# Start addresses in on-chip memory: pads at three places, and one product's moving operands set 32 bytes in front of a 128-byte boundary

## The reference, cut to what matters

```
u = rmsnorm(x, g_mix);  z = u @ w_in                        # mix: 2048 x 7184
y = concat(hgrn2 heads, gla heads)                          # gated recurrences, 12 heads
h = x + y @ w_out                                           # out: 2048 x 2048
m = rmsnorm(h, g_mlp) @ w_up                                # up: 2048 x 8192
h = h + square(relu(m)) @ w_down                            # down: 8192 x 2048
gate = sigmoid(rmsnorm(h, g_ple) @ w_pg)                    # gate: 2048 x 2048
h = h + gate * (p @ w_pp);  out = rmsnorm(h, g_final)
```

## Time and profile before

| | |
|---|---|
| median of three runs | 2427.51 us (2427.02 to 2428.92) |
| the profiled execution, its own time | 2428.29 us |
| its span | 2426.6 us |
| PE busy | 2393.7 us, 99% of the span, 13375 matmuls |
| weight loads (PEld) busy | 2082.1 us, 86% |
| DVE busy | 1939.1 us, 80% |
| ACT busy | 1202.9 us, 50% |
| granted TensorE clock | 0.998 of full speed (2.4 GHz) on the mean |

### The profile page before, as it was taken

How to read it: one execution, slowest core, us unless ns; L and a number is a source line. 1 busy time by engine, 2 the same in 40 slices (tenths; PEclk the granted TensorE clock), 3 DMA queues, 4 the chain that set the end, 5 groups by cost and what they waited for, 6 DMA issues and landing times.

```text
span 2426.6 us, 34798 instructions
## 1 busy us (share of the span) xinstructions
PE 2393.7 (99%) x13375; PEld 2082.1 (86%) x13375; DVE 1939.1 (80%) x2589; ACT 1202.9 (50%) x1787; POOL 50.7 (2%) x79
## 2 busy tenths in 40 slices
PE   8999999999999999999999999999999999999997
PEld 6888888888777888999999999988888888888885
DVE  6777777788887447988888888899999999995456
ACT  6445444444445235666666666643333333345345
POOL 4000000000000000000000000000000000000111
PEclk9999999999999999999999999999999999999999
DMA  6323323333324234666666666697564575633322
GB/s 176 87 73 82 86 70 85 87 84 81 79 74 152 92 131 137 182 204 200 199 197 196 197 196 196 205 353 253 198 232 160 191 257 195 229 131 116 112 85 99
DMA packets 381406, 373.71 MB, mean 154 GB/s; under 512 B 5532, under 2 KB 311352, under 8 KB 379224
## 3 DMA queue, kind: packets, MB, share of 16 engines
q1 hardware_dynamic: 381240, 371.88, 48.0%
q10 hardware_dynamic: 32, 0.01, 0.0%
HBM read 304.76 MB, written 67.11 MB: 153 GB/s over the span
## 4 chain that ended last, share of the span: by engine, by line
PE 62%; DVE 4%; ACT 1%; issue 1%; DMA 1%; DVEq 0%; ACTq 0%; SPq 0%
PE bank L2323 20%; PE bank L2325 20%; PE bank L2324 20%; DVE w_lo L2064 1%; DMA ring<-in_w_down 0%; DVE h L2110 0%; DVE w_lo L1927 0%; ACT w_hi L1143 0%; DVE w_lo L2201 0%; PE bank L2708 0%; PE bank L2603 0%; DVE gate_e L2227 0%; DVE h L2230 0%; PE bank L2401 0%; ACT gate_inv L1355 0%
## 5 line engine op out<-in xcount | busy, mean ns | idle before, releaser
L2323 PE MATMUL bank<-u_hi,w_hi 128*128 128x512 f32 x896 | 361.8, 404 | 3.4 <-DVE w_lo L1466 2.0
L2323 PE MATMUL bank<-w_hi,forms 128*128 128x512 f32 x896 | 349.4, 390 | 1.1 <-DVE h L2110 1.1
L2325 PE MATMUL bank<-u_hi,w_lo 128*128 128x512 f32 x896 | 349.8, 390 | 0.0
L2324 PE MATMUL bank<-u_lo,w_hi 128*128 128x512 f32 x896 | 349.2, 390 | 0.0
L2325 PE MATMUL bank<-w_hi,forms 128*128 128x512 f32 x896 | 348.7, 389 | 0.0
L2324 PE MATMUL bank<-w_lo,forms 128*128 128x512 f32 x896 | 348.6, 389 | 0.0
L2323 PE MATMUL bank<-xs,w_hi 128*128 128x256 f32 x1024 | 289.9, 283 | 1.4 <-DVE w_lo L1927 0.9
L2324 PE MATMUL bank<-xs,w_hi 128*128 128x256 f32 x1024 | 289.6, 283 | 0.0
L2325 PE MATMUL bank<-xs,w_lo 128*128 128x256 f32 x1024 | 289.5, 283 | 0.0
L1273 ACT ACTIVATE w_hi<-ring 128x1024 fp32r<-128x1024 f32 x124 | 132.0, 1066 | 214.6 <-PE bank L2325 140.4
L1466 DVE TENSOR_TENSOR w_lo<-w_raw,w_hi 128x2048 fp32r<-128x2048 f32 x70 | 160.0, 2286 | 63.2 <-ACT w_hi L874 63.0
(11 more groups left out here) (315 smaller groups left out, 5235.1 us busy)
## 6 DMA issues: line engine op xcount, KB each, us to landing
w_raw<-in_w_in SPq DMA_DIRECT2D x56, 1024.0 KB, 5.6
forms_scratch<-stage SPq DMA_DIRECT2D x32, 1792.0 KB, 11.4
forms<-forms_scratch SPq DMA_DIRECT2D x56, 1024.0 KB, 8.3
ring<-in_w_down SPq DMA_DIRECT2D x39, 1024.0 KB, 5.3
w_raw<-in_w_up SPq DMA_DIRECT2D x32, 1024.0 KB, 7.8
raw<-in_w_up SPq DMA_DIRECT2D x32, 1024.0 KB, 8.0
w_raw<-in_w_down SPq DMA_DIRECT2D x25, 1024.0 KB, 5.1
ring<-in_w_pg SPq DMA_DIRECT2D x18, 1024.0 KB, 5.0
```

Source lines behind the costliest of these rows:

```text
L2323: pe.matmul(ps, whi, xhi, start=start, stop=False, skip_group_check=shared)
L2324: pe.matmul(ps, whi, xlo, start=False, stop=False, skip_group_check=shared)
L2325: return pe.matmul(ps, wlo, xhi, start=False, stop=stop, skip_group_check=shared)
```

## The change: pads and offsets

A helper `aligned` allocates a byte tensor up to the next multiple of 128 that leaves at least 32 bytes of room in front. It is called ahead of u_hi, between u_hi and u_lo, and ahead of y. The tensors xs, xd and x11 of the up stage start 32 bytes (`SKEW`) in front of the regions' starts; xs gets a gap of 128 bytes between its two planes, so that the second starts 32 bytes in front of a multiple of 128 too. The other tensors laid out by `at` keep their offsets from region0 and region1, and move with them.

The pads before u_hi and between u_hi and u_lo move everything behind them by 128 and 256 bytes, from one multiple of 128 to another. The pad before y has 32 bytes and moves region1 from a remainder of 96 to 0. With remainders before and after as in the table above, every engine's instructions, their order and their waits are the same in both programs; only addresses differ.

```diff
+LINE, SKEW = 128, 32
...
-        region0 = -(-nc.sbuf_base // 64) * 64
+        def aligned(name, room):
+            start = -(-nc.sbuf_base // 32) * 32
+            end = -(-(start + room) // LINE) * LINE
+            if end > start:
+                sb(name, [P, end - start], U8)
+            assert nc.sbuf_base % LINE == 0
+            return nc.sbuf_base
+
+        region0 = aligned("pad0", SKEW)
         u_hi = sb("u_hi", [P, KT, S], F32R)
+        aligned("pad2", SKEW)
         u_lo = sb("u_lo", [P, KT, S], F32R)
...
-        region1 = nc.sbuf_base
+        region1 = aligned("pad1", SKEW)
         y = sb("y", [P, KT, S], stack=reg1)
...
-        xs = at("xs", region0, [P, 2, 4, 2, 2, 2, HALF], F32R)
-        xd = at("xd", region1, [P, 2, KT // 2, 2, HALF], F32R)
-        x11 = at("x11", region1 + KT * D, [P, KT // 2, 2, HALF], F32R)
+        xs = at("xs", region0 - SKEW, [P, 2, KT * S + LINE // 4], F32R)[:, :, 0:KT * S]\
+            .rearrange("q a (n j i l s) -> q a n j i l s", n=4, j=2, i=2, l=2)
+        xd = at("xd", region1 - SKEW, [P, 2, KT // 2, 2, HALF], F32R)
+        x11 = at("x11", region1 + KT * D - SKEW, [P, KT // 2, 2, HALF], F32R)
```

## The result

The changed kernel takes 2448.74 us (median of 6 runs, 2447.81 to 2451.48) against 2428.07 us before: ratio 1.0087, 95% interval 1.0077 to 1.0097. It is 20.7 us slower. The forecast was 2420.0 us with a range up to 2426. The profiled execution has a span of 2446.6 us against 2426.6.

The account below looks back on a forecast made before the run. The prediction took PE's pace, how fast one matmul follows another, as the bound. Up 4.5, gate 2.2 and mix 0.8 summed to 7.5 us off 2427.5, giving 2420.0 us, with an 8-in-10 range of 2416.5 to 2426.

Parts of the forecast that it names:

- u_hi, forms and all weight slots keep remainder 0: no change: Out and down stages: these operands' remainders stay 0, so no time was expected to change.
- the prediction's own sign of being right: Out and down must keep their lengths, 192 and 614 us, to within half a microsecond.
- a stationary operand at 96 costs 6.7 ns: Gate stage: steps with x1 or x2 at 96 take 233.3 ns a matmul, against 226.7 with x3 at 0.
- Up, 4.5 us: Up stage: xs going from 0 to 96 brings its products to 2.84 us, 4.5 us off over 32 pairs.
- Gate, 2.2 us: Gate stage: x1 and x2 going from 96 to 0 bring steps from 5.60 to 5.44 us, 2.2 us off.
- Mix, 0.8 us: Mix stage, float32 matmuls: 1.0 us gained by moving operands going to 0, less 0.2 for A at 32.
- the prediction's own sign of being wrong: Mix growing by more than 1 us, which would mean remainder 32 for A, V and norm costs the bounded 0.9.
- DVE, ACT, transfers at nothing: Vector and scalar work and transfers: addresses give 0, as small differences lie behind PE's work.
- the slower one: Rival: xs at 96 disturbs weight loads in up, up to 6.7 ns a matmul, 2445 us; chance 0.05.
- Nothing, by place in memory: Rival: pace depends on the part of memory a tensor lies in, not its remainder; 2427.5 us, chance 0.12.
- The rule of 16-byte lines: Whole kernel: remainders 0, 32 and 96 all start on a 16-byte line, so the time stays 2427.5 us.

Follow-up runs that it names:

- e1: The kernel before with one pad of 128 bytes in front of u_hi, so all tensors move up together: 2426.98 against 2428.25 us, ratio 0.9994.
- the second map: The kernel before with offsets and pads giving each stage another distance (mix -64, out +64, down +96, xd 0): 2447.11 us, ratio 1.0077.

## Why the prediction was wrong

- *Where it failed*: the step "u_hi, forms and all weight slots keep remainder 0: no change". The remainder was taken modulo 128 and of each operand alone. What counts is the difference of the two starts modulo 256 (in a stream whose matmuls all have the same one), and the pads of 128 and 256 bytes moved it from 0 to 128 for forms, x3 and u_hi. Down paid 13.8 us and out 4.4 (5.8 with the lower clock) where the sum had 0 and the prediction's own sign of being right was that both keep their length to half a microsecond. The readings of the rows were right, but the prediction read a rule of each operand's own remainder out of them ("a stationary operand at 96 costs 6.7 ns"), where they fit a distance of +32 and -32 as well. The kernel before had no float32r stream at a distance of 128, so its trace could neither show nor exclude this; the step took as given what it should have bounded, with 6.7 ns a matmul from the earlier trace rows on the 2688 of down, 18 us.
- *Up, 4.5 us*: right for the second plane of xs (2.84 us a product). The first plane went to a distance of +96, not -32, and stayed at 2.88. With both at -32 up lost 5.2 us (639.0 against 644.2).
- *Gate, 2.2 us*: x1 and x2 gained as said, 1.7 us when done alone. In the changed kernel x3 and p's tiles lost what they gained.
- *Mix, 0.8 us*: the stage grew by 2.6 us, the prediction's own sign of being wrong (more than 1 us), but for u_hi at 128 from w_hi and not for the float32 tiles. The streams lost more (229.0 against 227.3 ns a matmul, 4.6 us), and shorter waits gave part of it back (11.6 against 13.3 us). The gain from the float32 matmuls did not come: sixteen ql,kl take 1.95 us after the change as before it, where 1.92 was named. The term rested on a difference of 1.5 ns between 1.67 us over 15 distances (which is 111.3 ns, not 111.5) and 0.33 us over 3, and a row is rounded to 0.01 us, 3 ns in the second. Mix as a whole can't decide such a size: e1, which changes no distance, is 1.6 us shorter in mix than before as well, so differences of that size in this stage mean nothing.
- *DVE, ACT, transfers at nothing*: nothing speaks against it; DVE's busy time in up is 563.48 us in both kernels, and down came back to 614.5 us with forms alone set back.
- *The rivals*: the slower one named 2445 us, near the 2448.7 measured, but that is luck: its mechanism (xs disturbs the loads in up) is wrong, as up got faster. "Nothing, by place in memory" is refuted by xd in the second map and by xs at 2.84 in the low part of memory. The rule of 16-byte lines in the Trainium skill ("SBUF — State Buffer", Specifications (TRN2)) would have had the time unchanged; 0 against 128 bytes of distance, both multiples of 16, gave 5.44 and 5.58 us.

## What to carry to other kernels

A pad changes the distance between any two operands on either side of it, so check each pairing of moving and stationary operand, not each tensor, and modulo 256 (where two pairings alternate in a stream, measure it). If TensorE is the bound and its matmuls follow one another without a gap, compare the pace (start to start) with the same matmul elsewhere in the trace: two paces for one shape at one granted clock point to addresses. Compare the granted clock of each stage before a difference of 1 to 2 us is put down to the change. And when a stream gets faster, look at which wait it runs into next: here it was ScalarE's copy. In this kernel distance 0 is the best for 512 columns, and for 256 columns it is, with +96, the worst that was measured; the best version (2405.6 us) has 0 for the one and -64, with one product at -32, for the other.

## What the runs showed of the hardware

Pace of float32r matmuls with a weight load each, at 2.4 GHz, by distance in bytes, in streams where all matmuls have the same distance (from 24 or more start times each; over a product of 24 the first and last may carry a little of the neighbours):

```
512 columns   0: 226.7 ns    +64: 228.9    128: 232.4 (233.3 in parts of out)    -32, +32, -64, +96: 233.3    -96: 234.3
              -16: 226.7 or 233.3
256 columns   0, +96: 120.0    -48, -80: 119.2    128: 118.5 to 118.8    -32: 118.3    +32: 117.8
              -96: 117.3    +64, -64: 113.3 or 117.8
```

The best pace of both shapes is the same 17/16 of the columns: 226.7 ns are 544 cycles at 2.4 GHz for 512, and 113.3 ns are 272 for 256. The addresses of the two operands cost up to 7.6 ns a matmul over it, and what ran before can count too. That the reads of the moving and the stationary operand hinder each other fits this, but no run shows it.
